# Attention scores of a hybrid trunk kernel: two stacked products in place of three split ones

## The reference

```
proj = xn @ w_in                                   # q, k, v, u, gates
q = rmsnorm(q.reshape(b, l, 4, 64), q_norm_g);  k = rmsnorm(k.reshape(b, l, 4, 64), k_norm_g)
z = q.k / sqrt(64)                                 # only where key < query, else masked
log_keep = log_sigmoid(-z)
attn = exp(z + sum over keys between of log_keep)  # stick breaking
out = attn @ v                                     # per head
h = h + (sig(g_a)*(out @ w_attn_proj) + sig(g_s)*(ssm @ w_ssm_proj)) @ w_o
h = h + (silu(conv_g) * conv_v) @ w_down
```

## Time and profile before

| | us |
|---|---|
| median of three executions | 797.02 |
| the profiled execution | 793.84 |
| its span from first to last instruction | 792.1 |
| PE busy | 733.0 (93%) |
| PE weight loads busy | 698.9 (88%) |
| DVE busy | 461.8 (58%) |
| ACT busy | 290.2 (37%) |
| POOL busy | 170.2 (21%) |

### The profile page before, as it was taken

The page is one execution under the profiler, slowest core; times in us unless marked ns, Lnnn a source line. Parts: engine busy times, 40 slices in busy tenths (PEclk is TensorE's granted clock), DMA queues, the critical chain, the costliest instruction groups (busy, mean ns, idle before and its releaser), DMA issues.

```text
span 792.1 us, 13944 instructions
## 1 busy us (share of the span) xinstructions
PE 733.0 (93%) x5530; PEld 698.9 (88%) x5530; DVE 461.8 (58%) x641; ACT 290.2 (37%) x412; POOL 170.2 (21%) x195
## 2 busy tenths in 40 slices
PE   1897677899999999898999999999999999999997
PEld 1797576899899999898999999999999999888886
DVE  1987599856465685565448566665666665222211
ACT  1612111332254566553345343433434344121211
POOL 3539895570010000121320110011011011000000
PEclk9999779999889999999999999999999999999999
DMA  7325110324431111132322323323232233235431
GB/s 174 88 82 135 48 48 28 76 61 109 110 96 54 54 48 40 50 105 81 100 86 83 106 80 91 94 80 105 79 99 86 83 112 110 74 86 145 114 86 40
DMA packets 138868, 67.87 MB, mean 86 GB/s; under 512 B 23320, under 2 KB 137212, under 8 KB 138828
## 3 DMA queue, kind: packets, MB, share of 16 engines
q1 hardware_dynamic: 138668, 67.29, 30.8%
q10 hardware_dynamic: 160, 0.02, 0.0%
HBM read 61.85 MB, written 4.26 MB: 83 GB/s over the span
## 4 chain that ended last, share of the span: by engine, by line
PE 75%; DVE 14%; POOL 4%; ACT 3%; issue 2%; DMA 2%; SPq 0%; ACTq 0%; DVEq 0%; POOLq 0%
PE ps L1536 67%; DMA raw<-in_w_in_dram 2%; DVE lo L1040 1%; PE ps L1737 1%; DVE qT L1075 1%; PE ps L1712 1%; PE ps L1720 1%; PE ps L1653 1%; PE ps L1624 1%; DVE awl L1297 1%; ACT hi L748 1%; PE ps L1648 1%; ACT aw L861 1%; ACT aw L857 1%; DVE xl L1065 1%
## 5 line engine op out<-in xcount | busy, mean ns | idle before, releaser
L748 ACT ACTIVATE hi<-raw 128x1024 fp32r<-128x1024 f32 (+2 forms) x104 | 113.7, 1093 | 357.0 <-PE ps L1536 317.6
L1536 PE MATMUL ps<-xh,hi 128*128 128x258 f32 (+1 forms) x1120 | 232.5, 289 | 2.0 <-DVE xl L1065 1.0
L1536 PE MATMUL ps<-xh,lo 128*128 128x258 f32 (+1 forms) x1120 | 229.1, 286 | 0.0
L1536 PE MATMUL ps<-xl,hi 128*128 128x258 f32 (+1 forms) x1120 | 228.9, 286 | 0.0
L1040 DVE TENSOR_TENSOR lo<-raw,hi 128x1024 fp32r<-128x1024 f32 (+2 forms) x104 | 138.9, 1336 | 129.9 <-ACT hi L748 129.5
L1536 PEld LDWEIGHTS ps<-xh,hi 128*128 128x128 f32 x1120 | 177.2, 193 | 4.7 <-DVE lo L1040 1.7
L1536 PEld LDWEIGHTS ps<-xl,hi 128*128 128x128 f32 x1120 | 177.0, 192 | 0.0
L1536 PEld LDWEIGHTS ps<-xh,lo 128*128 128x128 f32 x1120 | 177.0, 193 | 0.0
L731 POOL TENSOR_TENSOR cv<-cv 128x512 f32<-128x512 f32 x22 | 28.3, 1286 | 230.3 <-DVE cv L1494 230.3
L1494 DVE SCALAR_TENSOR_TENSOR cv<-ut,cols,cv 128x512 f32<-128x512 f32 x88 | 65.9, 748 | 6.4 <-ACT cv L990 0.9
L1536 PE MATMUL ps<-ah,hi 128*128 128x512 f32 x176 | 69.2, 393 | 0.0
(11 more groups left out here) (284 smaller groups left out, 1023.3 us busy)
## 6 DMA issues: line engine op xcount, KB each, us to landing
raw<-in_w_up_dram SPq DMA_DIRECT2D x88, 256.0 KB, 3.1
raw<-in_w_in_dram SPq DMA_DIRECT2D x52, 256.0 KB, 3.3
raw<-in_w_down_dram SPq DMA_DIRECT2D x16, 384.0 KB, 3.4
raw<-in_w_down_dram SPq DMA_DIRECT2D x16, 320.0 KB, 4.1
raw<-in_w_o_dram SPq DMA_DIRECT2D x16, 256.0 KB, 2.9
raw<-in_w_ssm_proj_dram SPq DMA_DIRECT2D x8, 256.0 KB, 2.9
out_dram<-yt SPq DMA_DIRECT2D x8, 256.0 KB, 2.4
xtok<-in_x_dram SPq DMA_DIRECT2D x1, 1056.0 KB
```

The lines of the kernel that those rows point to most:

```text
L748: act.activation(hi[slot][:, 0:n * P], raw[slot][:, 0:n * P], ACT.Copy)\
L1536: ins = pe.matmul(o, weights[w], acts(a, c), start=start and i == 0, stop=stop and i == 2)
```

## The change

The rows of the weights are now used fully. For head `h`, `k2[h%2]` holds k high in the head's own 64 rows and k low in the other 64. `qh2[h%2]` holds q high twice, once in each half, and `ql2[h%2]` q low twice. One matmul with `qh2` then adds high by high and low by high; one with `ql2` adds high by low and low by low. Each region has two matmuls and not three, and the zeros of POOL and their semaphore are gone. ACT and DVE prepare each head by itself: three instructions of 64 rows each on either engine (one for k, two for q, of which one writes into the other half of the rows than it reads), so six per pair of heads where there were three. PE waits for its own head's k (`kl_set` at `h + 1`).

```diff
--- before.py
+++ after.py
@@ -241,15 +241,15 @@
         pad2 = alloc(scr, "pad2", [P, 3 * KS * L + 2 * ATT_COLS - 2 * KD * LL + 16])
         heads = ExitStack()
         awl = alloc(heads, "awl", [P, ATT_COLS], F32R)
-        qzl = [alloc(heads, f"qzl{i}", [P, LL], F32R) for i in range(2)]
-        kh = alloc(heads, "kh", [P, L], F32R)
-        kl = alloc(heads, "kl", [P, L], F32R)
+        ql2 = [alloc(heads, f"ql2{i}", [P, LL], F32R) for i in range(2)]
+
+        k2 = [alloc(heads, f"k2{i}", [P, L], F32R) for i in range(2)]
         heads.close()
         sh = alloc(scr, "sh", [P, KS, L], F32R)
         sl = alloc(scr, "sl", [P, KS, L], F32R)
         gt = [alloc(scr, f"gt{i}", [P, L]) for i in range(2)]
 
-        qzh = [alloc(scr, f"qzh{i}", [P, LL], F32R) for i in range(2)]
+        qh2 = [alloc(scr, f"qh2{i}", [P, LL], F32R) for i in range(2)]
         scr.close()
         mix.close()
 
@@ -325,7 +325,6 @@
         ss_v = sem("ss_v")
         rs_a = sem("rs_a")
         normed = sem("normed")
-        qz_zero = sem("qz_zero")
         kh_set = sem("kh_set")
         kl_set = sem("kl_set")
         qh_set = sem("qh_set")
@@ -385,6 +384,11 @@
 
             return ps[part, bank:bank + 2, 0:width]
 
+        def halves_of(h):
+
+            own = DH * (h % 2)
+            return slice(own, own + DH), slice(DH - own, P - own)
+
         def halves(ap, width):
             return ap.rearrange("p (b c) -> p b c", c=width)
 
@@ -705,14 +709,6 @@
                     if name == "prep" and 1 <= i < ROUNDS - 1:
                         input_map(i + 1)
                         output_map(i + 1)
-                    if name == "readout" and i + 1 == ROUNDS:
-
-                        pool.wait_ge(y_ps, ROUNDS)
-                        pool.wait_ge(yg_set, ROUNDS)
-                        for part, i in ((slice(DH, P), 0), (slice(0, DH), 1)):
-                            for q in (qzh[i], qzl[i]):
-                                link(pool.memset(q[part, :].bitcast(F32), 0.0))
-                        pool.nop().then_inc(qz_zero, 1)
             for m in range(KD):
                 pool.wait_ge(m_gated, m + 1)
                 pool.tensor_tensor(ma[m % 2][:], ma[m % 2][:], mb[m % 2][:], ALU.add)\
@@ -831,23 +827,19 @@
                                ACT.Gelu_apprx_tanh).then_inc(yg_set, 1)
                 act.preload_act_table_set("natural_log_exp_and_others")
                 if r == ROUNDS - 1:
-                    act.wait_ge(qz_zero, 1)
-                    head_k(0)
-                    head_q(0)
-                    head_q(1)
-
-            def head_k(t):
-                act.wait_ge(normed, 4)
-                if t:
-                    act.wait_ge(z_ps, 2 * t)
-                act.activation(kh[:], kT[:, t], ACT.Copy).then_inc(kh_set, 1)
-
-            def head_q(h):
+                    act.wait_ge(normed, 4)
+                    head(0)
+                    head(1)
+
+            def head(h):
+
+                own, other = halves_of(h)
                 if h >= 2:
                     act.wait_ge(z_ps, h - 1)
-                part = slice(DH * (h % 2), DH * (h % 2) + DH)
-                act.activation(qzh[h % 2][part, :], qT[part, h // 2, 0:LL], ACT.Copy)\
-                    .then_inc(qh_set, 1)
+                act.activation(k2[h % 2][own, :], kT[own, h // 2], ACT.Copy).then_inc(kh_set, 1)
+                for part in (own, other):
+                    ins = act.activation(qh2[h % 2][part, :], qT[own, h // 2, 0:LL], ACT.Copy)
+                ins.then_inc(qh_set, 1)
 
             def scores(h):
                 for two in (BANKS[0:2], BANKS[2:4]):
@@ -868,9 +860,8 @@
 
             def suffix(h):
                 if h == 1:
-                    head_k(1)
-                    head_q(2)
-                    head_q(3)
+                    head(2)
+                    head(3)
                 act.wait_ge(suf_ps, h + 1)
                 act.wait_ge(soft_lo, AB * h + AB)
                 for b in range(AB):
@@ -1273,21 +1264,21 @@
 
             def readout(r):
                 if r == ROUNDS - 1:
-                    head_k(0)
-                    head_q(0)
-                    head_q(1)
-
-            def head_k(t):
-                dve.wait_ge(kh_set, t + 1)
-                dve.tensor_tensor(kl[:], kT[:, t], kh[:].bitcast(F32), ALU.subtract)\
+                    head(0)
+                    head(1)
+
+            def head(h):
+
+                own, other = halves_of(h)
+                dve.wait_ge(kh_set, h + 1)
+                dve.tensor_tensor(k2[h % 2][other, :], kT[own, h // 2],
+                                  k2[h % 2][own, :].bitcast(F32), ALU.subtract)\
                    .then_inc(kl_set, 1)
-
-            def head_q(h):
                 dve.wait_ge(qh_set, h + 1)
-                part = slice(DH * (h % 2), DH * (h % 2) + DH)
-                dve.tensor_tensor(qzl[h % 2][part, :], qT[part, h // 2, 0:LL],
-                                  qzh[h % 2][part, :].bitcast(F32), ALU.subtract)\
-                   .then_inc(ql_set, 1)
+                for part in (own, other):
+                    ins = dve.tensor_tensor(ql2[h % 2][part, :], qT[own, h // 2, 0:LL],
+                                            qh2[h % 2][own, :].bitcast(F32), ALU.subtract)
+                ins.then_inc(ql_set, 1)
 
             def scores(h):
 
@@ -1674,7 +1664,7 @@
 
             def scores(h):
 
-                pe.wait_ge(kl_set, h // 2 + 1)
+                pe.wait_ge(kl_set, h + 1)
                 pe.wait_ge(ql_set, h + 1)
                 for bank in BANKS:
                     if bank == 0:
@@ -1683,9 +1673,9 @@
                             pe.wait_ge(s_, n)
                     mine = [g for g in REGIONS if g[0] == bank]
                     for n, (_, c0, kb, q0, q1) in enumerate(mine):
-                        for i, (kk, qq) in enumerate(((kh, qzh), (kh, qzl), (kl, qzh))):
+                        for i, qq in enumerate((qh2, ql2)):
                             ins = pe.matmul(ps[:, 4 + bank, c0:c0 + q1 - q0],
-                                            kk[:, KEY0[kb]:KEY0[kb] + P],
+                                            k2[h % 2][:, KEY0[kb]:KEY0[kb] + P],
                                             qq[h % 2][:, q0 - LATE0:q1 - LATE0],
                                             start=n == 0 and i == 0, stop=False,
                                             skip_group_check=True)
```

## The result

The first timing gave 807.43 us (806.52, 808.52, 808.34, 798.32) against 796.91 us, a ratio of 1.0118 with a 95% interval of 1.0072 to 1.0165. Twelve more executions of the same kernel gave a median of 799.77 us beside 799.37 us of before, 0.9998 (0.9951 to 1.0045). One kernel scatters over 14 us here, which the three times at the start did not show. Both together, the changed kernel has a mean of 802.3 us (16 runs, standard error 1.3), the one before 799.0 us (51 runs, those of a copy among them, error 0.6). In such kernels the change costs +3.6 +- 1.1 us on one chip (+3.1 +- 1.0 without the slowest of its twelve runs) and +2.4 +- 1.0 us on another: 0.3 to 0.5%. Ratios leave out executions over 1.5% above the fastest of their kernel; means take in all but the few over 1000 us.

What follows compares the result with a forecast made beforehand. It took the DVE and ACT chain ahead of the suffix steps as the bound, not PE: of 3.4 us PE removed, 0.63 us gained, added work 0, 797.02 - 0.63 = 796.4 us. Own range 795.6 to 797.0, wider range 793.5 to 799.8.

Steps and rivals of the forecast that it cites:

- The matmuls removed, heads 1 to 3: Scores of heads 1 to 3: 0.84 us less PE per head, of which 0.63 us in all reach the end.
- The cap by `attl`: Heads 1 to 3: DVE is busy with the previous head's `attl`, so only about 0.22 of 0.48 us per head is gained.
- Preparation of heads 0 and 1: Ahead of scores(0): four POOL memsets go, three ACT and three DVE instructions come; six copies fit without cost.
- added work 0: Term of the sum: the extra ACT and DVE head-preparation copies add 0 us to the time.
- Hidden, with 0.5 us to spare: Ahead of scores(0): DVE's copies end at 225.6, before its next work at 226.09.
- The pauses: PE's waits ahead of the suffix steps grow to about 2.06 us for head 0, 1.1 us for the others.
- rival 2: Clock falls behind the 2.06 us pause ahead of suffix(0): net 798.0 to 801.3 us, likeliest 798.4; chance 0.15.
- the upper of the two (4.9): Price of a clock fall from one readout and product: 9.64 us at full clock, 14.56 us at mean 0.65.
- the lower (1.6): Price of a clock fall from another stretch, 7.10 against 8.68 us at 0.80; called likeliest since dense work follows.
- Rival 1: All 3.4 us of removed PE matmul time is gained: 793.6 us; chance 0.06.
- 3: Rival: the clock falls at all four suffix steps, 5.8 us slower, 802.8 us; chance 0.02.
- rival 4: Head preparation does not fit, by double-time writes into the other half or ACT and DVE hindering each other: 800 us; chance 0.04.

Runs made afterwards that it cites:

- e2: The kernel before, unedited, run again: median 797.58 us, ratio to before 0.9983.
- e4: The changed kernel with a third matmul per region again (q low added twice), so only the new head preparation differs from before: median 803.21 us, ratio 1.0028.
- e1: The changed kernel, unedited, run again: median 799.77 us, ratio to before 0.9998.
- i4: The changed kernel with head 1's copies moved to suffix(0) and spare matmuls in PE's other pauses, none ahead of suffix(0): mean 795.4 us, ratio to before 0.9991.
- e3: The kernel before without its third score product (k low by q high), old head preparation kept: median 799.08 us, ratio to before 0.9984.
- i2: The changed kernel with spare matmuls in PE's pauses, 16 of them ahead of suffix(0): mean 792.4 us, ratio to before 0.9960.
- i1: The changed kernel with spare matmuls in PE's other pauses, the one ahead of suffix(0) left whole: mean 796.2 us, ratio to before 1.0012.
- i3: The kernel before with spare matmuls in PE's other pauses, its 1.22 us pause ahead of suffix(0) left whole: mean 792.6 us, ratio to before 0.9959.
- f2: The changed kernel with a first set of spare matmuls in ten PE pauses, suffix(0) included: 796.20 us, one run.
- f1: The kernel before with a first set of spare matmuls in ten PE pauses, suffix(0) included: 797.28 us, one run.
- g1: The changed kernel with 16 spare matmuls ahead of suffix(0) and nothing else: mean 797.9 us, ratio to before 0.9987.

## Why the prediction was wrong

- **The matmuls removed, heads 1 to 3.** On the chain, right: 0.34 us for head 1 and 0.52 us for the other two together (21.89 less 21.55, 43.78 less 43.26), 0.86 us in all against 0.63 forecast. The cap by `attl` is as told; the overlap of 0.07 us was missing. On PE, wrong: the 0.84 us per head came, nearly, for head 0 alone (2.91 to 2.10 us). For the others PE now waits 0.34 us for `attl` ahead of bank 0, which the forecast did not have, and the step shrinks by 0.35 us, not 0.84. This costs nothing on the chain, and it keeps the later pauses short (see below).
- **Preparation of heads 0 and 1: the first step that failed.** The sum has "added work 0". "Hidden, with 0.5 us to spare" took the end of unit 18's product from a profile in which that stretch ran at a PEclk of 0.65. At full clock the product ends 2 us sooner against the copies (room 0.15 us, e2). DVE took up the evacuation 0.20 us behind the first matmul of `scores(0)` in e2 (225.23, 225.03); in the changed kernel this would be 231.27, and it was 232.68, 1.41 us late. From there to the split it took 1.15 us in e2, a wait of 0.46 us for ACT among it, and 0.61 us now: 0.54 us are covered, and 0.87 us are left, the 0.86 us of the stage. So 0.86 us gained and 0.86 us lost: the stages' sum is nothing. e4, which has the new copies and three products, shows the same 0.86 us by themselves. The row that gave the cover was itself the product of a fall; its clock stood beside it in the earlier trace rows.
- **The pauses.** Ahead of suffix(0) 2.06 us were forecast; it is 2.91 us with the late copies added, and 2.04 to 2.08 where they are not late or the third product is back. Ahead of the other three about 1.1 us were forecast, and it is 0.51, 0.64 and 0.51 us, hardly more than before (0.49, 0.45, 0.49): PE's new wait takes up what was to lengthen them.
- **The pause put at nothing: the second step that failed, and the larger.** The sum gives the longer pause no cost and leaves the fall of the clock to rival 2, with a chance of 0.15. It was the likeliest case: the clock fell at this point in five of seven profiles with a pause of 2.0 us or more and in none of eleven with 1.24 us or less. Place and kind were right. The price was 4.7 us in four profiles, near the upper of the two (4.9) and not at the lower (1.6) that was called likeliest, and 6.1 us in the first, above both. The prediction counted the one long pause that held (2.33 us) and called the fall at 1.53 us a matter of narrow matmuls behind it. The late copies are not needed for the fall: in e1 and i4 it came behind 2.04 us, as long as the pause that was forecast.
- **Rival 1, 3 and 4.** Not all was gained, and only this one of the four suffix steps had a fall. A write into the other half takes 0.70 us like any other, as the earlier trace rows had it; 0.72 us from start to start held for all six. So rival 4 had the right place, ahead of `scores(0)`, for a wrong reason.
- **The measured change.** 10.5 us, where rival 2 had 4.3 us at most: 3 of 4 runs fell, by chance, on the upper end of a distribution 14 us wide. With the twelve runs of e1 (median 799.77 us) the time would have lain just inside the forecast's range, by luck and not by its account. The bound of 0.5% for what a measurement tells was too small for four runs of a kernel whose standard deviation is 4 us; three executions 3.7 us apart hid that.

What stays open: whether two products of the kind in e3, with old copies, are slower than before. Its profile kept the clock behind 2.06 us, and three of its twelve runs lie above 806 us. And no run shows why the clock falls behind one pause of 2.04 us and not behind another of 2.06.

## What to carry to other kernels

Read the margin of a step that is to hold more work from a stretch at full clock; one measured where the matmul engine ran slow is not there in an execution in which it runs fast. Matmul time removed ahead of a wait can become a longer pause, and where that pause grows past what the kernel had, its clock may fall and cost more than the matmuls did: spare matmuls in the pause are a cheap test and, here, a gain (i2 against i1, 3.8 us). Where one kernel scatters by 14 us, compare stretches between fixed instructions before comparing medians.

## What the hardware showed beside this

- Falls of the clock make most of the scatter. Filling the pauses of before but that ahead of `suffix(0)` brought the spread from 15 us (789.8 to 805.0, 35 runs) to 3.1 us (i3, 12 runs) and took 6.3 us off the mean on that chip, for 176 spare matmuls, some 21 us of PE at 0.12 us each.
- A fall is a matter of chance at a given pause: behind the unfilled 1.53 us ahead of readout(3) the clock fell in four of seven profiles, in the first of before and not in its second, and behind 2.20 to 2.23 us ahead of `state(1)` in one of five.
- The stretch from `state(1)` to `readout(1)` takes 17.2 us in three profiles (before, e2, e3) and 19.6 us in the other 15, which are of either kernel. In the 15, DVE's 264-column products take 1.23 to 1.34 us, not 0.43, while POOL runs products of its own beside them. f2:

```profile
158.61 1.25 DVE L1242 TENSOR_TENSOR mod<-mod,rot 128x264 f32<-128x264 f32 x1
159.78 1.33 DVE L1243 TENSOR_TENSOR mod<-mod,rot 128x264 f32<-128x264 f32 x1
...
158.46 1.10 POOL L410 TENSOR_TENSOR g_in<-pw,bb 128x512 f32<-128x512 f32 x1 [7.52 <-PE ps L1608]
```

and e3, where POOL starts at 160.98 us and the same two DVE lines are through:

```profile
159.61 0.44 DVE L1251 TENSOR_TENSOR mod<-mod,rot 128x264 f32<-128x264 f32 x1
159.97 0.43 DVE L1252 TENSOR_TENSOR mod<-mod,rot 128x264 f32<-128x264 f32 x1
```

In e3 too the product that begins beside POOL takes long (DVE's at 161.24 us, 1.33 us). No run takes POOL's products away, so that they are the cause is inferred from this coincidence.

- What decides the order is, in these profiles, a fall of the clock that helps. In the three short ones, and in no other, the clock had fallen at `state(1)`, behind pauses of 3.01, 2.20 and 3.01 us (mean PEclk 0.90 in the stretch, 0.99 to 1.00 in the 15). POOL, which waits for a product of PE, starts 5.0 us behind DVE's first product of the step there, and 3.5 us behind it in the others. In the six long ones without spare matmuls ahead of `readout(1)` (after, e1, e4, f1, f2, g1), PE then waits 3.7 us for `kern`, the clock falls behind it, and the way to `readout(3)` takes 48.5 to 48.7 us instead of 43.9. These 2.3 and 4.8 us are 7.1 of the 9.83 us by which the first profile after came late to `readout(3)`. f1, a kernel before, has them as well.
